# Two transformer blocks in one launch: the orders of work behind LayerNorms and in the first attention, changed

## The reference, cut to what matters

```python
def reference(x, ...):            # x: 1 x 512 x 1024, float32
    x = first_block(x, ...)
    return second_block(x, ...)

# first_block: RMSNorm; layer 0 hybrid attention, layer 1 differential attention; gated FFN with a causal conv
ob = forgetting_attention(heads(qb) * scale, heads(kb), heads(vb), logf)
#   logit[t,s] = q_t.k_s + sum_{s<j<=t} log f_j, causal, 8 heads of 64
# second_block: twice
h = layer_norm(DN_ALPHA * h + mix, ln1_g[l], ln1_b[l])       # mix: conv, gated linear attention, MLA, conformer conv
h = layer_norm(DN_ALPHA * h + conv_ffn(h, ...), ln2_g[l], ln2_b[l])
# cos, sin of MLA's rotation from positions (integers) x inverse frequencies, once
```

## Time and profile before

| | us |
|---|---|
| median of 3 runs | 2573.56 (2569.62 to 2573.78) |
| the profiled execution, its own time | 2574.53 |
| its span, first to last instruction | 2572.6 |
| TensorE busy | 2474.2 (96%) |
| VectorE busy | 1699.2 (66%) |
| ScalarE busy | 1024.6 (40%) |
| GpSimd busy | 1007.9 (39%) |

### The profile page before, as it was taken

How to read it: one execution, slowest core, us unless ns; L and a number is a source line. 1 busy time by engine, 2 the same in 40 slices (tenths; PEclk the granted TensorE clock), 3 DMA queues, 4 the chain that set the end, 5 groups by cost and what they waited for, 6 DMA issues and landing times.

```text
span 2572.6 us, 33482 instructions
## 1 busy us (share of the span) xinstructions
PE 2474.2 (96%) x11222; PEld 1904.8 (74%) x11222; DVE 1699.2 (66%) x2241; ACT 1024.6 (40%) x1628; POOL 1007.9 (39%) x431
## 2 busy tenths in 40 slices
PE   7999999999999999999899899999999989999997
PEld 5676787888777678888677467788777746778876
DVE  7654775587777678176788557818767855781875
ACT  4444432222344532133564644313346464431333
POOL 2222444444310044444454044444455404453444
PEclk9999999999999999999999999999999999999999
DMA  5212232223322233223222022323322202232222
GB/s 170 77 63 58 82 98 98 90 94 102 99 86 83 62 98 100 89 97 105 67 94 66 11 72 82 102 86 98 100 72 93 67 9 74 82 99 89 96 97 77
DMA packets 65342, 217.48 MB, mean 85 GB/s; under 512 B 8416, under 2 KB 8672, under 8 KB 65120
## 3 DMA queue, kind: packets, MB, share of 16 engines
q1 hardware_dynamic: 64384, 214.79, 26.0%
q10 hardware_dynamic: 864, 1.44, 0.2%
HBM read 207.81 MB, written 2.10 MB: 82 GB/s over the span
## 4 chain that ended last, share of the span: by engine, by line
PE 78%; DVE 8%; issue 6%; ACT 4%; POOL 3%; DVEq 0%; ACTq 0%; DMA 0%; POOLq 0%; SPq 0%
PE bank_G L670 23%; PE bank_G L672 22%; PE bank_G L671 22%; POOL wlo L560 3%; DVE conv_up L1112 2%; ACT whi L641 1%; DVE prod L1132 1%; PE bank_S L1712 1%; PE bank_S L2228 1%; PE bank_X L1740 1%; PE bank_O L1964 1%; PE bank_O L1726 1%; PE bank_S L1953 1%; DVE conv_up L1111 1%; DVE conv_up L1110 1%
## 5 line engine op out<-in xcount | busy, mean ns | idle before, releaser
L560 POOL TENSOR_TENSOR wlo<-raw,whi 128x1024 fp32r<-128x1024 f32 (+2 forms) x361 | 905.2, 2509 | 1513.9 <-ACT whi L641 1488.8
L670 PE MATMUL bank_G<-n_hi,whi 128*128 128x512 f32 x2248 | 903.1, 402 | 42.0 <-DVE n_lo L966 20.8
L672 PE MATMUL bank_G<-n_hi,wlo 128*128 128x512 f32 x2248 | 881.2, 392 | 0.0
L671 PE MATMUL bank_G<-n_lo,whi 128*128 128x512 f32 x2248 | 880.8, 392 | 0.0
L641 ACT ACTIVATE whi<-raw 128x1024 fp32r<-128x1024 f32 (+2 forms) x389 | 403.5, 1039 | 602.5 <-PE bank_G L672 602.2
L670 PEld LDWEIGHTS bank_G<-n_hi,whi 128*128 128x128 f32 x2248 | 425.6, 189 | 159.1 <-DVE n_lo L966 27.2
L672 PEld LDWEIGHTS bank_G<-n_hi,wlo 128*128 128x128 f32 x2248 | 425.3, 189 | 91.6
L671 PEld LDWEIGHTS bank_G<-n_lo,whi 128*128 128x128 f32 x2248 | 425.8, 189 | 88.0 <-issue 4.8
L670 PE MATMUL bank_G<-a_hi,whi 128*128 128x512 f32 x704 | 276.6, 393 | 8.5 <-DVE a_lo L1134 3.9
L672 PE MATMUL bank_G<-a_hi,wlo 128*128 128x512 f32 x704 | 274.1, 389 | 0.0
L671 PE MATMUL bank_G<-a_lo,whi 128*128 128x512 f32 x704 | 274.0, 389 | 0.0
(11 more groups left out here) (342 smaller groups left out, 2706.5 us busy)
## 6 DMA issues: line engine op xcount, KB each, us to landing
raw<-in_w_mix_in SPq DMA_DIRECT2D x40, 512.0 KB, 3.3
raw<-in_w_hyb_in SPq DMA_DIRECT2D x25, 512.0 KB, 3.3
raw<-in_w_diff_in SPq DMA_DIRECT2D x24, 512.0 KB, 3.3
raw<-in_w_up0a SPq DMA_DIRECT2D x22, 512.0 KB, 3.3
raw<-in_w_up0b SPq DMA_DIRECT2D x22, 512.0 KB, 3.3
raw<-in_w_up1a SPq DMA_DIRECT2D x22, 512.0 KB, 3.3
raw<-in_w_up1b SPq DMA_DIRECT2D x22, 512.0 KB, 3.3
raw<-in_w_up2a SPq DMA_DIRECT2D x22, 512.0 KB, 3.3
```

The source lines that it names most:

```text
L560: pool.tensor_tensor(b.wlo[:, g.slot, w], b.raw[:, g.slot, w], b.whi[:, g.slot, w], ALU.subtract).then_inc(b.lo_ready, 1)
L670: pe.matmul(out, b.whi[:, g.slot, w], hi[:, hi_at + k, :], start=(k == 0), stop=False)
L671: pe.matmul(out, b.whi[:, g.slot, w], lo[:, lo_at + k, :], start=False, stop=False)
L672: mm = pe.matmul(out, b.wlo[:, g.slot, w], hi[:, hi_at + k, :], start=False, stop=(k == pieces - 1))
```

## The change

ScalarE, TensorE and VectorE get other orders at the ramps (`ramp_slice_pe`, `chunk` with `gated`, `tile(2)` ahead of the gates' exponential); VectorE centres slices 0 and 1 of each LayerNorm from bank_O instead of GpSimd; the forget rows go to DRAM once and come back spread over the partitions by eight transfers on ScalarE's queue; the angles are computed in seven pieces, each behind a residual add of the down product.

```diff
--- before.py
+++ after.py
@@ -93,7 +93,7 @@
 POST_HYB = 0
-POST_DIFF = POST_HYB + 8 + 64 + 8
+POST_DIFF = POST_HYB + 8 + 64
 POST_NORM = POST_DIFF + 8 + 32
 POST_MIX = POST_NORM + 8
@@ -375,7 +375,11 @@
     b.out_taken = sem("out_taken")
     b.fox = sem("fox")
+    b.dve_centred = sem("dve_centred")
     b.fox_masked = sem("fox_masked")
+    b.fox_out = sem("fox_out")
+    b.fox_in = sem("fox_in")
+    b.fox_rows = nc.dram_tensor("fox_rows", (8, T), F32, kind="Internal").ap()
     b.lam = sem("lam")
     b.sub_sq = sem("sub_sq")
     b.sub_rs = sem("sub_rs")
@@ -694,13 +698,29 @@
+def ramp_slice_pe(pe, b, g, k, ready):
+    if k == 0:
+        pe.wait_ge(b.lo_ready, g.at(1))
+        wait(pe, b.evacuated, g.at(-1))
+    out, w = b.G[:, g.slot, :], slice(k * P, (k + 1) * P)
+    pe.wait_ge(b.nhi_ready, ready)
+    pe.matmul(out, b.whi[:, g.slot, w], b.n_hi[:, k, :], start=(k == 0), stop=False)
+    pe.matmul(out, b.wlo[:, g.slot, w], b.n_hi[:, k, :], start=False, stop=False)
+    pe.wait_ge(b.nlo_ready, ready)
+    mm = pe.matmul(out, b.whi[:, g.slot, w], b.n_lo[:, k, :], start=False, stop=(k == KD - 1))
+    if k == KH - 1:
+        mm.then_inc(b.half_free, 1)
+    if k == KD - 1:
+        mm.then_inc(b.gemm_done, 1)
 def ramp_gemms_n(pe, b, name, nlo):
     g0 = FIRST[name]
     for k in range(KD + TRAIL):
         if k < KD:
-            pe.wait_ge(b.nlo_ready, nlo + k + 1)
-            gemm(pe, b, Index(g0), b.n_hi, b.n_lo, KD, None, range(k, k + 1), half=(k == KH - 1))
+            ramp_slice_pe(pe, b, Index(g0), k, nlo + k + 1)
         if k >= TRAIL:
             gemm(pe, b, Index(g0 + 1), b.n_hi, b.n_lo, KD, None, range(k - TRAIL, k - TRAIL + 1))
@@ -860,6 +880,9 @@
         act.activation(square_at(b, x, k), b.h[:, k, :], ACT.Square).then_inc(b.shift_squared, 1)
+CENTRED = 2
 def normed_bank(b, k):
     return (b.X[:, 0, :], b.X[:, 1, :], b.O[:, 1, :], b.S[:, 1, :])[k % 4]
@@ -867,7 +890,7 @@
 def norm_centre_pool(pool, b, x):
     pool.wait_ge(b.mean_taken, x.n + 1)
-    for k in range(KD):
+    for k in range(CENTRED, KD):
         h = b.h[:, k, :]
         pool.wait_ge(b.shift_squared, 8 * x.n + k + 1)
         pool.tensor_tensor(h, h, b.mean[:, :], ALU.subtract).then_inc(b.centred, 1)
@@ -977,9 +1000,15 @@
         dve.wait_ge(b.plain_summed, 8)
         variance = dve.tensor_tensor(b.rstd[:, :], b.rstd[:, :], b.mixed[:, 1], ALU.add)
     variance.then_inc(b.variance_ready, 1)
+    for k in range(CENTRED):
+        dve.wait_ge(b.shift_squared, 8 * n + k + 1)
+        dve.scalar_tensor_tensor(h[k], b.O[:, 0, :], -1.0 / D, h[k], ALU.mult, ALU.add).then_inc(b.dve_centred, 1)
     dve.wait_ge(b.scale_ready, 2 * n + 2)
     for k in range(KD):
-        dve.wait_ge(b.centred, 8 * n + k + 1)
+        if k < CENTRED:
+            dve.wait_ge(b.dve_centred, CENTRED * n + k + 1)
+        else:
+            dve.wait_ge(b.centred, (KD - CENTRED) * n + k - CENTRED + 1)
         if k >= 4:
             dve.wait_ge(b.h_ready, 8 * n + k - 3)
         dve.scalar_tensor_tensor(normed_bank(b, k), h[k], v_(b, x.gain, k), b.S[:, 0, :], ALU.mult,
@@ -1072,7 +1101,7 @@
     g0, tiles = group_tiles(name)
     scaled = c0 < 2 * FC
-    def chunk(g, g_next, c, j, width, width_next, ramp=False):
+    def chunk(g, g_next, c, j, width, width_next, ramp=False, gated=False):
         if scaled:
             split_hi(act, b, g.after(2), width)
             split_hi(act, b, g_next.after(2), width_next)
@@ -1081,20 +1110,28 @@
             act.wait_ge(b.prod_done, c + 1)
             act.activation(b.a_hi[:, j, :], b.prod[:, :], ACT.Copy).then_inc(b.act_hi, 1)
             return
-        wait(act, b.conv_done, c)
-        take(act, b, g, b.gate[:, PAD:PAD + T], width=width, ramp=ramp)
+        if not gated:
+            wait(act, b.conv_done, c)
+            take(act, b, g, b.gate[:, PAD:PAD + T], width=width, ramp=ramp)
         wait(act, b.prod_done, c)
         take(act, b, g_next, b.up[:, PAD:PAD + T], width=width_next)
         act.wait_ge(b.conv_done, c + 1)
         act.activation(b.silu[:, :], b.conv[:, :], ACT.Silu).then_inc(b.silu_done, 1)
+        if ramp:
+            act.wait_ge(b.conv_done, c + 1)
+            take(act, b, g.after(2), b.gate[:, PAD:PAD + T], width=W8)
         act.wait_ge(b.prod_done, c + 1)
         act.activation(b.a_hi[:, j, :], b.prod[:, :], ACT.Copy).then_inc(b.act_hi, 1)
     if not scaled:
         act.wait_ge(b.evacuated, g0)
     chunk(Index(g0), Index(g0 + 1), c0, 0, W8, W8, name in RAMPS)
-    with act.Fori(0, HC - 2) as i:
-        chunk(Index(g0 + 2, i), Index(g0 + 3, i), c0 + 1 + i, bass.ds(i + 1, 1), W8, W8)
+    first = 1
+    if name in RAMPS:
+        chunk(Index(g0 + 2), Index(g0 + 3), c0 + 1, 1, W8, W8, gated=True)
+        first = 2
+    with act.Fori(0, HC - 1 - first) as i:
+        chunk(Index(g0 + 2 * first, i), Index(g0 + 2 * first + 1, i), c0 + first + i, bass.ds(i + first, 1), W8, W8)
     chunk(Index(g0 + tiles - 2), Index(g0 + tiles - 1), c0 + HC - 1, HC - 1, None, None)
@@ -1171,8 +1208,10 @@
                    f"conv_b{f}" if first_block else None, f"conv_w{f}" if first_block else f"dw_gate{f - LAYERS}",
                    None if first_block else f"dw_up{f - LAYERS}")
         if f == 0 and half == 0:
-            rope2_dve(dve, b, link)
-        if half == 0:
+            for m in range(KD):
+                residual_dve(dve, b, Index(FIRST["down0a"] + m), m)
+                rope2_dve(dve, b, link, m)
+        elif half == 0:
             products_dve(dve, b, f"down{f}{tag}", 1.0 if first_block else ALPHA)
         elif norm:
             for m in range(KD):
@@ -1613,11 +1652,8 @@
             if 0 <= step - self.lag < self.units:
                 order += [("att", step - self.lag, x) for x in range(2)]
             order += [("in", n) for n in follows(self, step)]
-            if self.fox_pair(step) is not None:
-                order += [("fox", self.fox_pair(step), x) for x in range(2)]
         order = count_posts(self, post, order)
         self.posts = [[post + order.index(("att", u, x)) for x in range(2)] for u in range(self.units)]
-        self.fox_posts = {o: [post + order.index(("fox", o, x)) for x in range(2)] for o in range(4, 8)}
     def unit(self, u):
         return u // NB, NB - 1 - u % NB
@@ -1643,6 +1679,7 @@
 ATT_HYB = HybridPairs(POST_HYB)
+FOX_ROWS_STEP = 8
 class DifferentialHeads:
@@ -1741,16 +1778,6 @@
         mm.then_inc(b.posted, 1)
-def hyb_fox_pe(pe, b, a, o):
-    pe.wait_ge(b.fox, 5)
-    for x in range(2):
-        p, n = Index(a.fox_posts[o][x]), 2 * o + x - 8
-        pe.wait_ge(b.x_free[p.slot], p.turn())
-        pe.matmul(b.X[:, p.slot, :], b.k["ident"][0:8, n:n + 1].to_broadcast([8, P]), b.negc[0:8, :],
-                  start=True, stop=True).then_inc(b.posted, 1)
 def hyb_attention_pe(pe, b):
     a = ATT_HYB
     for step in range(a.steps):
@@ -1762,8 +1789,6 @@
         if 0 <= t < a.units:
             hyb_transposes_pe(pe, b, a, t)
         inputs_pe(pe, b, a, step)
-        if a.fox_pair(step) is not None:
-            hyb_fox_pe(pe, b, a, a.fox_pair(step))
         m = step - a.out_step
         if 0 <= m < KD:
             out_first_pe(pe, b, OUT_HYB, m)
@@ -1819,11 +1844,15 @@
         inputs_act(act, b, a, step)
         if a.tiles.index(("f", 0)) in a.ends.get(step, ()):
             forget_log_act(act, b, link)
-        if a.fox_pair(step) is not None:
+        o = a.fox_pair(step)
+        if step == FOX_ROWS_STEP:
+            act.wait_ge(b.fox, 5)
+            act.dma_start(b.fox_rows, b.negc[0:8, :]).then_inc(b.fox_out, 16)
+        if o is not None:
+            act.wait_ge(b.fox_out, 16)
             for x in range(2):
-                p = Index(a.fox_posts[a.fox_pair(step)][x])
-                act.wait_ge(b.posted, p.at(1))
-                act.activation(fox_mask(b, a.fox_pair(step))[:, x], b.X[:, p.slot, :], ACT.Copy).then_inc(b.x_free[p.slot], 1)
+                n = 2 * o + x - 8
+                act.dma_start(fox_mask(b, o)[:, x], b.fox_rows[n:n + 1, :].partition_broadcast(P)).then_inc(b.fox_in, 16)
         if 0 <= step - a.out_step < KD:
             split_hi(act, b, Index(outa + step - a.out_step + 2))
@@ -1874,8 +1903,7 @@
         if 4 * NB <= v < a.units:
             o, i = a.unit(v)
             if v % NB == 0:
-                for x in range(2):
-                    taken_out(dve, b, Index(a.fox_posts[o][x]))
+                dve.wait_ge(b.fox_in, 32 * (o - 3))
             dve.wait_ge(b.masked, 2 * v)
             block = fox_mask(b, o)[:, :, i * P:(i + 1) * P]
             corner = b.k["causal"][:, (NB - 1) * P:].rearrange("p (a c) -> p a c", a=1).to_broadcast([P, 2, P])
@@ -2122,23 +2150,27 @@
 SIN_MAX = 3.1415925
-def rope2_dve(dve, b, link):
-    dve.wait_ge(b.vec_in, 16)
-    dve.wait_ge(b.rare_in, 16 * RARE_LOADS)
...
+def rope2_dve(dve, b, link, part):
+    if part == 0:
+        dve.wait_ge(b.vec_in, 16)
+        dve.wait_ge(b.rare_in, 16 * RARE_LOADS)
```

(36 more changed lines are left out.)

## The result

The kernel after takes 2552.1 us (median of 4 runs, 2551.3 to 2552.5), before 2572.9 (4 runs, 2569.6 to 2573.8): ratio 0.9915, interval 0.9903 to 0.9928, 20.8 us less. The forecast was 18.4 less, 2556.1: the sign was right, the time is 4.0 us lower, in the range. Of these 4.0, 1.6 come from the start of the sum: it began at the profiled execution's 2574.53, and the median of before is 2572.9. The change itself is 2.4 larger than forecast. The profiled execution took 2551.28 us, its span 2549.3, so the two profiles differ by 23.3.

A forecast was written before the change was run, and what follows sets the result against it. TensorE, busy 96% of the span, was taken as the bound. Terms 7.6 + 2.8 + 2.8 + 2.4 + 1.8 + 1.0 = 18.4 us, taken from the profiled 2574.53, gave 2556.1 us; range 2551.5 to 2561.5.

The forecast's parts named there:

- Forget rows by transfers: First attention: four pairs of products leave TensorE, 1.90 us each, the added transfers stay hidden; 7.6 us less (4 to 7.6).
- Angles in pieces: First down product: with the residual add ahead, TensorE's 2.68 us wait goes; 2.8 us less, lower bound 2.0.
- High halves first: Four LayerNorm ramps: TensorE starts on n_hi 0, 0.85 us earlier; 0.7 us a ramp, 2.8 in all (1.8 to 3.4).
- the prediction's lower case: LayerNorm ramps: if the low clock ends where it did, the earlier start is worth 0.45 us a ramp.
- Centring: LayerNorms: two slices centred by VectorE, hidden in the ramps; last norm's scaling ends earlier, 2.4 us less (1.4 to 2.45).
- ScalarE's order in the up stages: Two up stages: tile 4's pause of 1.64 us goes, part returns at tile 6; 0.9 each, 1.8 in all (0 to 3.3).
- 0.5 to 1.5: Sign of being right: the 1.4 us pause at tile 4 gone, one of this many us at tile 5 or 6.
- ScalarE's order in the mixers: Two mixers: tile 4's pause goes, tile 5 waits for its split; 0.5 us each, 1.0 in all (-1.5 to 3.2).
- The clock that returns sooner: Rival, behind the norms: full clock returns earlier, 2.5 us a ramp instead of 0.7 in two of four; 2552.5 us, chance 0.17.
- Bound first attention: Rival, first attention: VectorE and ScalarE can't follow at 24.97 us, the 7.6 us are lost; 2563.7 us, chance 0.07.
- late broadcasts: Rival, first attention: the spread forget rows land slowly, holding VectorE and TensorE; 2581 us at 25 us a pair, chance 0.03.
- the moved pauses: Rival, up stages and mixers: pauses for wlo only move, neither order change keeps anything; 2558.9 us, chance 0.20.

The follow-up runs named there:

- after again: The kernel after, unchanged, timed beside before in five rounds: 2552.5 us, ratio 0.9919 (0.9906 to 0.9933).

## Why the prediction was right or wrong

**The step that failed** is in the terms of the forget rows and of the angles: both price a piece of TensorE's time at its length alone and put the half clock behind it at nothing. The sum also multiplied up2a's ramp by four and so had no term for the first ramp's own cause.

**Forget rows by transfers**: "So 4 x 1.90 = 7.6 us go" holds to 0.1 (TensorE's groups). The transfers hid: they landed in 3.4 to 5.8 us and had 18.7. Not in the term: the half clock behind one of the pairs, 1.6 us in 6 of 7 profiles, and perhaps a part of the stretch at 228. Measured 8.8 to 9.5.

**Angles in pieces**: the pause's 2.8 is measured 2.9. Not in the term: the half clock that followed the pause in 4 of 7 profiles (1.3 on average), and 1.2 at the first ramp from the unrolled loop, of which nothing in the profile of before speaks except that L978 took 1.66 us. I had read only up2a's ramp and multiplied by four; the first one's wait was 6.62 against 4.79 and had this cause in it.

**High halves first**: forecast 0.7 a ramp, measured 0.69 in each wait, not 0.85, since TensorE starts 0.16 after n_hi ends. How much of it is left at the ramp's end goes with the half clock behind the restart. In up2a that was 4.6 us and is 5.7 in after, in up3a 5.2 and 5.9, and the 48th matmul comes at 13.42 and 13.54 instead of 13.00 and 13.26: 0.3 and 0.4 are left, the prediction's lower case. In the second mixer's ramp it fell from 5.8 to 4.5 us, and the gate product comes at 15.90 instead of 16.57 behind the restart: 1.4 are kept. The average of 0.7 is right, the single ramps are not.

**Centring**: hidden in the ramps (VectorE's idle before the first scaling 1.42, now 0.23) and 2.4 at the tail, as forecast.

**ScalarE's order in the up stages**: 0.9 forecast, 0.7 measured. With the high halves the prediction has 1.6 for ramp and stage; measured are 1.0 to 1.2. The two gains do add (0.3 or 0.4 and 0.7); what is missing is what the clock took in the ramp and the 0.2 of this term. The pause moved to tile 6 with 0.78, within the 0.5 to 1.5 named.

**ScalarE's order in the mixers**: 0.7 each instead of 0.5; tile 5's pause is 0.71 and VectorE took nothing back.

**The sum.** The three parts without a term come to 1.6 x 6/7 + 1.3 + 1.2 = 3.9 us. The change is 2.4 larger than forecast (2.0 in the rounds of after again), so some 1.5 us of the opposite sign are not accounted for; the medians of before themselves lie between 2572.9 and 2574.2 from one set of rounds to the next. That the time came near the lower end of the range is partly luck of that kind.

**Rivals.** The clock that returns sooner named 2552.5, nearly the time measured, by a mechanism that isn't it. Behind the four restarts together half clock lasts 19.2 and 20.2 us in the two profiles of before and 19.5 and 20.3 in the two of after; in up2a's ramp the stretch is as long as before, 6.8 us. In the first ramp one profile of after has it half as long as the other, with TensorE's wait for probs at the mixer's end 193.05 and 193.09 us after the restart. So the full clock comes back about 0.7 earlier, with the restart, and not the rival's 2.5. The mechanism itself exists: a stretch of half the length stands behind 7 of the 36 ramps with the early start and behind 1 of the 28 without, and behind up3a it was worth 1.2 us. By the Trainium skill's rule (TensorE: Matmul & The Clock Gate, "What's actually happening") activity releases the throttle; these traces agree as far as the early restart goes with an early return on average. Bound first attention and late broadcasts didn't come; the moved pauses kept 0.7 a place.

## What to carry to other kernels

Before pricing a pause or a thin product of TensorE, read the granted clock behind it in several executions: here a pause of 2.2 to 2.7 us cost its length plus 0 to 3.0 us. Measure a stage from a point behind the ramp as well as from the restart: the order's 0.7 was the same in every profile from there, while from the restart the clock blurred it (1.0 alone, 0.3 to 0.5 with the high halves). And an order that removes pauses can lose at the stage's end: here it paid once the consumer behind the stage took the last slice last (2557 became 2539.5 by that).

## What was not expected of the hardware

- Half clock (1.2 GHz) for 3.4 us behind one of four pairs of float32 products over 8 rows, which kept TensorE busy without a gap (197.09 above); which pair changes with the execution.
- The same wait of 2.23 us is followed by half clock or not, by execution (0.72 or 1.00 as mean of 6 us); half clock follows it only where an earlier stretch (24 us, or behind a product pair) had come, in 9 of 16 profiles.
- The same VectorE operation on SBUF took 0.69 or 1.66 us (TENSOR_TENSOR, first ramp) and 0.48 or 3.45 (TENSOR_SCALAR, up stage) beside GpSimd. In the ramp a start 0.2 us earlier goes with the short time and the writing out of a loop of eight adds, 850 us before, goes with the early start, in 10 profiles against 6.
